# Moving work between three engines in the attention loops of a hybrid decoder trunk

## The reference, cut to what matters

```python
for layer in range(DEPTH):
    h = rms_norm(x, ln1_g[layer])
    (a_q, a_ckv, ..., b_u, c_q, c_kv, c_gate) = jnp.split(h @ w_in[layer], offsets, axis=-1)
    a_out = dsa_mixer(...)     # _, sel = lax.top_k(score, k_top), k_top = 64
    b_out = s5_mixer(...)      # y = gelu(Re(C h) + D u);  y * sigmoid(y @ glu_w + glu_b)
    c_out = nsa_mixer(...)
    x = x + mixed @ w_out[layer]
    z = rms_norm(x, ln2_g[layer]) @ w_up[layer]
    x = x + jnp.square(jax.nn.relu(z)) @ w_down[layer]
```

## Time and profile before

| | us |
|---|---|
| median of 3 runs | 635.5 (634.96 to 637.03) |
| profiled execution | 635.55 |
| its span, first to last instruction | 633.8 |
| PE busy | 611.7 (97%) |
| DVE busy | 437.0 (69%) |
| ACT busy | 360.5 (57%) |
| POOL busy | 237.8 (38%) |

### The profile page before, as it was taken

The page is one execution under the profiler, slowest core; times in us unless marked ns, Lnnn a source line. Parts: engine busy times, 40 slices in busy tenths (PEclk is TensorE's granted clock), DMA queues, the critical chain, the costliest instruction groups (busy, mean ns, idle before and its releaser), DMA issues.

```text
span 633.8 us, 10302 instructions
## 1 busy us (share of the span) xinstructions
PE 611.7 (97%) x3798; PEld 505.8 (80%) x3798; DVE 437.0 (69%) x785; ACT 360.5 (57%) x639; POOL 237.8 (38%) x418
## 2 busy tenths in 40 slices
PE   7989989999999999999999999999999999999996
PEld 6867866688888888888888787668888888888885
DVE  7699887396756767895676877637776654665664
ACT  5855689736546444444375658984654553554452
POOL 5899678504031999960005206871000000000001
PEclk9999999999999999999999999999999999999999
DMA  9674804165965655466638640414576656656631
GB/s 255 206 205 134 162 8 113 42 184 156 293 209 190 198 171 195 148 197 227 195 94 280 118 123 3 118 35 132 140 261 199 189 176 199 199 172 194 197 102 66
DMA packets 55436, 102.73 MB, mean 162 GB/s; under 512 B 12713, under 2 KB 18906, under 8 KB 55354
## 3 DMA queue, kind: packets, MB, share of 16 engines
q1 hardware_dynamic: 49130, 96.30, 50.3%
q0 software_dynamic: 1792, 4.07, 2.8%
q10 hardware_dynamic: 4464, 1.70, 1.1%
HBM read 99.69 MB, written 1.31 MB: 159 GB/s over the span
## 4 chain that ended last, share of the span: by engine, by line
PE 80%; POOL 6%; ACT 5%; DVE 5%; issue 2%; DMA 1%; SPq 0%; POOLq 0%; DVEq 0%; ACTq 0%
PE pb L1799 77%; ACT tab_zone L1172 2%; POOL dtmp L840 1%; DVE sc_zone L1687 1%; DMA raw<-in_w_in 1%; ACT w_hi L926 1%; POOL yz L621 1%; PE pb L1953 1%; PE pb L1825 1%; POOL sp L621 1%; DVE w_lo L1371 1%; ACT ptmp L1186 1%; PE pb L2219 1%; POOL w_lo L801 1%; DVE tab_zone L1292 1%
## 5 line engine op out<-in xcount | busy, mean ns | idle before, releaser
L1371 DVE TENSOR_TENSOR w_lo<-raw,w_hi 128x1024 fp32r<-128x1024 f32 (+2 forms) x176 | 221.6, 1268 | 124.3 <-ACT w_hi L926 123.5
L926 ACT ACTIVATE w_hi<-raw 128x1024 fp32r<-128x1024 f32 (+2 forms) x184 | 188.0, 1027 | 188.3 <-PE pb L1799 174.4
L1799 PE MATMUL pb<-h_both,w_hi 128*128 128x512 f32 x512 | 181.7, 399 | 0.0
L1799 PE MATMUL pb<-h_both,w_lo 128*128 128x256 f32 x512 | 143.7, 281 | 0.0
L1799 PE MATMUL pb<-w_hi,h_both 128*128 128x512 f32 (+2 forms) x448 | 128.0, 370 | 5.3 <-DVE w_lo L1371 5.2
L1799 PEld LDWEIGHTS pb<-h_both,w_hi 128*128 128x128 f32 x512 | 96.2, 188 | 24.2 <-issue 0.6
L1799 PE MATMUL pb<-w_hi,z_hi 128*128 128x512 f32 (+1 forms) x260 | 101.0, 388 | 0.4 <-DVE w_lo L1371 0.4
L1799 PE MATMUL pb<-w_lo,z_hi 128*128 128x512 f32 (+1 forms) x260 | 100.5, 387 | 0.0
L1799 PE MATMUL pb<-w_hi,z_lo 128*128 128x512 f32 (+1 forms) x260 | 100.5, 386 | 0.0
L1799 PEld LDWEIGHTS pb<-h_both,w_lo 128*128 128x128 f32 x512 | 96.7, 189 | 0.5
L1799 PEld LDWEIGHTS pb<-w_hi,h_both 128*128 128x128 f32 x448 | 78.9, 188 | 20.1 <-DVE w_lo L1371 6.9
(11 more groups left out here) (315 smaller groups left out, 801.5 us busy)
## 6 DMA issues: line engine op xcount, KB each, us to landing
raw<-in_w_up SPq DMA_DIRECT2D x64, 512.0 KB, 4.1
raw<-in_w_down SPq DMA_DIRECT2D x64, 512.0 KB, 3.4
raw<-in_w_in SPq DMA_DIRECT2D x24, 512.0 KB, 4.3
raw<-in_w_out SPq DMA_DIRECT2D x8, 512.0 KB, 3.6
raw<-in_w_out SPq DMA_DIRECT2D x16, 256.0 KB, 4.9
raw<-in_w_in SPq DMA_DIRECT2D x8, 308.0 KB, 4.0
raw<-in_w_in SPq DMA_DIRECT2D x8, 280.0 KB, 2.9
x<-in_x ACTq DMA_DIRECT2D x4, 256.0 KB, 4.7
```

What stands on the lines that cost most here:

```text
L926: hi_made.by(act.activation(w_hi[:, n % RING, 0:width(n)], raw[:, n % RING, 0:width(n)], ACT.Copy))
L1371: lo_made.by(dve.tensor_tensor(w_lo[:, n % RING, 0:width(n)], raw[:, n % RING, 0:width(n)], w_hi[:, n % RING, 0:width(n)].bitcast(F32), AL ...
L1799: return pe.matmul(o, l, r, start=start, stop=stop, skip_group_check=True)
```

## The change

Four edits:
1. In layer 0, `s5_states_back` leaves DVE and is run by POOL, between `keys_w` and `gates`, with a new signal `scanned` for the two scans. Layer 1 keeps it on DVE.
2. In layer 0, one of the two rounds of maxima of slot 2 goes to slot 0, which then has two.
3. In both layers, turned y is read from PSUM by DVE, in slot 7 (`y_read`), and not by ACT. In layer 0 it stands ahead of `c_probs`, in layer 1 `c_probs` is a slot earlier.
4. In layer 1, POOL makes the low part of piece 22 behind slot 6, not slot 3.

```diff
-        LO_OUT = (None, 1, 3, 7)
+        LO_OUT = ((None, 1, 3, 7), (None, 1, 6, 7))
...
+                def s5_states_back():
+
+                    P0, P1, P3 = (t.rearrange("p (i n) -> p i n", i=2)
+                                  for t in (dtmp[:, 4], dtmp[:, 5], proj[:, 1, O_U - 256:O_U + 256]))
+                    c2, s2 = (rot[:, i].rearrange("p j c -> p (j c)").unsqueeze(1).to_broadcast([PART, 2, SEQ])
+                              for i in range(2))
+                    pool.wait_ge(scanned.sem, 2)
+                    tt(P0, P3, c2, ALU.mult, False)
+                    tt(P1, P3, s2, ALU.mult)
+                    Q = [P.rearrange("p i (j c) -> p i j c", j=PAIRS)[:, :, :, 0:NC - 1] for P in (P0, P1)]
+                    tt(ez[:, 0, :, 1:NC], Q[0][:, 0], Q[1][:, 1], ALU.subtract, False)
+                    ez_made.by(pool.tensor_tensor(ez[:, 1, :, 1:NC], Q[1][:, 0], Q[0][:, 1], ALU.add))
+                    pool.wait_ge(ez_made.sem, ez_made.at(L, 1))
+
                 keys_w()
+                if L == 0:
+                    s5_states_back()
                 gates()
...
-                    if p in LO_OUT:
-                        lo_out(20 + LO_OUT.index(p))
+                    if p in LO_OUT[L]:
+                        lo_out(20 + LO_OUT[L].index(p))
...
-                    if p == 6:
-                        act.wait_ge(yk_ps.sem, yk_ps.at(L, 1))
-                        yk_sb.by(act.activation(yg, pb[7][:], ACT.Copy))
-                        yk_half.by(act.activation(yt, pb[7][:], ACT.Copy, scale=0.25))
...
-                        step(dve.tensor_tensor_scan(P[3][:, i], d, P[2][:, i], 0.0, ALU.mult, ALU.add), i == 1)
+                        m = dve.tensor_tensor_scan(P[3][:, i], d, P[2][:, i], 0.0, ALU.mult, ALU.add)
+                        if L == 0:
+                            scanned.by(m)
+                        else:
+                            step(m, i == 1)
...
+                def y_read():
+
+                    dve.wait_ge(yk_ps.sem, yk_ps.at(L, 1))
+                    yk_sb.by(dve.tensor_copy(yg, pb[7][:]))
+                    yk_half.by(dve.tensor_scalar(yt, pb[7][:], 0.25, None, ALU.mult))
+
...
-                              19: (s5_lags, s5_sums_read, s5_states, index_sum, s5_states_back)}
+                              19: (s5_lags, s5_sums_read, s5_states, index_sum)}
...
-                for p, work in ((3, y_cube), (4, y_gelu), (5, c_max), (6 + D, c_probs), (9, y_glu)):
+                for p, work in ((3, y_cube), (4, y_gelu), (5, c_max), (7, y_read), (6 + D, c_probs), (9, y_glu)):
                     between[p].append(work)
-                for p in ((0, 1, 2, 2, 3, 4, 5, 6) if L == 0 else (0, 0, 2)):
+                for p in ((0, 0, 1, 2, 3, 4, 5, 6) if L == 0 else (0, 0, 2)):
                     between[p].append(top)
```

More of the change, by code:

```diff
@@ L339, in trunk @@
         xs_read = sig("xs_read", 1)
-        ez_made = sig("ez_made", 1)
+        scanned, ez_made = sig("scanned", 0), sig("ez_made", 1)
         rk_ps = sig("rk_ps", 1)
```

## The result

| | before | after |
|---|---|---|
| median, first comparison | 635.71 (634.96 to 637.42, 7 runs) | 633.20 (632.82 to 634.20, 7 runs) |
| second comparison | 635.90 (25 runs) | 634.43 (632.77 to 636.49, 10 runs) |
| third | 635.94 (23 runs) | 633.89 (632.39 to 639.94, 11 runs) |
| profiled execution / span | 635.55 / 633.8 | 633.19 / 631.5 |

What follows compares the result with a forecast made beforehand. PE, busy for 97% of the span, was taken to bound the kernel. Gains of 0.4 us in layer 0 and 0.8 in layer 1, 1.2 off 635.5, gave 634.3; own range 634.1 to 635.1, 8-in-10 range 632.9 to 636.0.

Steps and rivals of the forecast that it cites:

- part 2: Layer 0, a maximum from slot 2 to slot 0: sc of slot 4 stays, sc of slot 5 gains 0.5 us.
- part 3: DVE reads turned y, 1.3 us: layer 0 keeps 0.4 of a 0.5 us gain; in layer 1 the reads cost nothing.
- the 0.4 of the sum: Layer 0's gain in us as taken for the forecast, with bounds 0 and 0.5.
- three signs of failure: Four S5 operations over 6.6 us; PE waiting for c_probs in layer 0's slot 8; layer 1's last transposes waiting for non-POOL.
- Part 1: Layer 0's S5 states on POOL: four operations take 4.0 us there, cost nothing, and alone gain nothing.
- the forecast 0.5 of waiting: Layer 0, sc of slot 5 loses its 0.51 us wait and goes to where DVE is free, 94.57.
- a cover of 0.1 us: Layer 0: c_probs ends at 104.95, PE turns its result at 105.08 when 0.5 early.
- Part 4: Layer 1, piece 22's low part from slot 3 to 6: last transposes go as POOL ends; 0.8 us taken.
- The bound of 0.9: Layer 1's upper gain in us, last transposes at 420.2 to 420.3; 0.4 if pn of slot 6 doesn't start earlier.
- all counts: Rival: all time taken away in both layers, 3.7 us, is gained, giving 631.8; chance 0.12.
- the waits move elsewhere: Rival: layer 0 gains 0 as c_probs is late for PE, layer 1 gains 0.4, giving 635.1; chance 0.20.
- POOL is held up: Rival: layer 0's four S5 operations take 11.6 us on POOL; 5.0 lost, 0.8 gained, giving 639.7; chance 0.08.

Runs made afterwards that it cites:

- e7: Kernel before with only layer 0's S5 states moved to POOL: 635.79 us, ratio 0.9979.
- e12: Kernel before with only the low part of layer 1's piece 22 moved to behind slot 6: 634.72 us (1 run).
- e13: Kernel before with one maximum of layer 0 moved from slot 2 to slot 0 and the table's loads issued ahead of the weights: 634.51 us (1 run).
- e2: Kernel before with turned y read by DVE in both layers and layer 1's piece 22 behind slot 6: 635.59 us, ratio 0.9990.
- e8: Changed kernel with two more 512-column products on DVE in slot 0 of layer 0: 634.65 us (1 run).
- e5: Kernel before, unchanged, profiled and timed again: 635.67 us.
- e9: Kernel before with the loads of layer 0's table of lags issued ahead of the weights on SP's queue: 636.94 us, ratio 0.9992.
- e14: Changed kernel with the table's loads first and two more products on DVE behind slot 2's scores in layer 0: 635.63 us.
- e10: Changed kernel with the loads of layer 0's table of lags issued ahead of the weights on SP's queue: 633.64 us, ratio 0.9938.
- e11: Changed kernel with the table's loads first and one more product on DVE behind slot 2's scores in layer 0: 634.63 us (1 run).
- e15: Changed kernel, unchanged, a third time: 633.89 us over eleven runs.
- e4: Changed kernel with the low part of layer 1's piece 22 behind slot 5 instead of 6: 633.70 us, ratio 0.9950.
- e16: Changed kernel with the table's loads first and layer 1's piece 22 in slot 5: 632.91 us, ratio 0.9940.

## Why the prediction was wrong in layer 0, and what in it was right

The step that failed is part 2's path through slots 3 and 4 of layer 0: sc of slot 4 "at 91.3, as before", and from there a gain of 0.5 us, less 0.1 for part 3. The measured loop gained 0.95 us for the 0.4 of the sum, 0.80 of it at the same lateness. Layer 1 gained 1.11 for 0.8, with the mechanism right and the size too small.

**What bounds the kernel, and the mechanisms.** These held. PE's wait before the scores of slot 4 went from 1.44 to 0.24; the last transposes of layer 1 are released by POOL; POOL has no gap from piece 22 on. None of the three signs of failure that it named came; they looked at POOL's price, c_probs and the end of layer 1, and none at the step that failed.

**Part 1** by itself gave nothing where it was tried, with a late table (e7, against e12), at 3.98 us for the 4.0. That it is only room for part 2 was right too; it is worth 0.44 where the table is early (e13).

**Part 2** is the step that failed. It had DVE's cube wait for ACT's square of y, which doesn't move, and so sc of slot 4 where it was. ACT hardly moved, but the square, which ended at 89.13, had not been what the cube waited for. Timeline of DVE in the kernel before, the cube in slot 3 and sc of slot 4:

```profile
89.36 0.68 DVE L1299 SCALAR_TENSOR_TENSOR yz<-yz,pb 128x512 f32<-128x512 f32 x1
...
91.34 0.28 DVE L1687 CUSTOM_DVE_ANT_0 sc_zone<-pb,cmask 128x128 f32<-128x128 f32 x1
```

The cube starts at 89.36 with no bracket: it stood in DVE's own queue, behind slot 3's sc, and that queue is what the change shortens. In after it has a bracket, 0.91 for ACT, and starts at 89.02, 0.34 earlier: 0.20 of the 0.23 us that lay between the square's end and the cube's start, and 0.14 because the square itself was that much earlier, as PE was (its product with the table at 80.81 and not 80.94). The same 0.33 stands at sc of slot 4 (91.01 for 91.34). The sum hid it: cube and top are 1.98 us in this timeline, from 89.36 to 91.34, where 0.65 and 1.45, 2.10, had been added to 89.13 and came out near the old time. DVE then took 3.15 us to sc of slot 5, where 3.23 had passed before, and the forecast 0.5 of waiting went as well: 94.16, 0.92 before the 95.08 of the earlier trace rows, and 0.93 of it reached the last transposes. The loop, by the table above, takes 37.43 us in the kernel before with a lateness of 0 or 0.33, and 36.75 and the lateness with 1.26 or 1.47 (e7, e12); the two meet at about 0.7, an estimate, as no profile lies between. In the changed kernel it is 36.30 and the lateness. At before's own 0.33 that is a gain of 0.80, twice the 0.4 of the sum, of which 0.1 had been taken off for part 3. With a late table it is 0.45, near the size forecast, but by luck: in e12 DVE stood 0.73 us for PE ahead of sc of slot 2, so the late table had already given DVE time.

**Part 3** was right in its price (0.66 and 0.68, for 1.3) and wrong in what it uses up: 0.1 was taken off for a cover of 0.1 us ahead of PE's turning of c_probs. c_probs ended at 104.50, 0.45 us earlier than forecast, after sc of slot 5 that was 0.41 earlier than forecast; PE, at 104.64, didn't wait for it, and e2 shows 21.96 against 21.97. In layer 1, too, it is nothing (e12).

**Part 4** went as told to a tenth: in before's time pn of slot 6 is at 407.74 (407.75 forecast), piece 22 at 409.68 (409.7), pn of slot 7 at 412.02 (412.05). The last transposes are at 420.06, where 420.2 was worked out and 0.8 taken of the 0.97 that it meant. It measured 1.11; the difference is 0.14 of overlap between POOL's operations, and the rounding down. The bound of 0.9 was too tight for a sum over six operations. The later load of piece 26 cost nothing that shows: from the last transposes to the end of the span it is 212.68 us for 212.63.

**The rivals.** That all counts (631.8) didn't come, nor that the waits move elsewhere (635.1). That POOL is held up (639.7) didn't come either, and e8 gives the price beside two wide products on DVE: 4.73 us for the four operations, below its point of 6.6.

**What the prediction did not weigh** is that executions of the kernel before differ by what happens in this very stretch. With an early table its layer 0 has a wait of 1.67 to 1.77 us before the scores of slot 4, and the clock over 90 to 95 us was then 0.66 in two of three profiles (e5, e2; not in e9), which cost 1.56 us (38.99 against 37.43). It was 1.00 in e14 with 1.83, and in all 14 with 1.44 or less. So the wait alone doesn't decide it. Something sets e2 and e5 apart from e9 and e14 that the experiments left untried: an earlier fall of the clock. (e9's expectation named a late start of the layer as a rival; e2 and e5 came to slot 1 at 79.25 and 79.32 us, e9 and e14 at 78.44 and 78.72.) The window from 10 us on, in e5 and then in e9:

```profile
core 0: us, PE busy (x) PEld busy (x) DVE busy (x) ACT busy (x) POOL busy (x), PEclk, DMA share, GB/s
10.00:15.00 5.00, 3.34 (x11) 2.57 (x10) 4.37 (x8) 5.00 (x11) 3.96 (x10) 0.68 1.22 306
```

```profile
core 0: us, PE busy (x) PEld busy (x) DVE busy (x) ACT busy (x) POOL busy (x), PEclk, DMA share, GB/s
10.00:15.00 5.00, 3.07 (x13) 2.55 (x14) 4.60 (x8) 5.00 (x11) 3.88 (x10) 1.00 1.22 299
```

Six of the 18 profiles have a clock below 1.00 somewhere in 10 to 20 us: after, e2, e5, e10, e11 and e15. Both falls at 90 us are among these, with the long wait. The other four of them waited 0.24 to 1.10 us, and e9 and e14 had the long wait without the earlier fall; in none of these six did the clock fall over 90 to 95 us. That would fit a cause that needs both, but two profiles of each kind don't show it, and no run tried it. The timed runs don't settle it either. e9 against e10, on one chip, looks like a fall in half of the executions that have the wait. But on e14's chip four of e14's ten runs had a granted clock of 0.995 or less, and so did five of e15's eleven, which don't have the wait. A run's clock doesn't tell where it fell; in after, e4 and e16 it was 0.94, 0.85 and 0.73 over 625 to 630 us.

What the profiles do show is 0.45 to 1.13 us in layer 0, by the lateness of the table, and 1.0 to 1.1 in layer 1, 1.5 to 2.3 together. The medians give 2.5, 1.5 and 2.0 us; the first is above this, and the three intervals (1.7 to 4.7, 0.8 to 3.9 and 0.4 to 3.6 us) reach into it. How much of the rest is the clock stays open.

## What to carry to other kernels

When work leaves an engine, ask of each later operation whether it waited for another engine or for its own queue; the bracket in the trace tells only the last to come, and an operation without a bracket stood in its own queue and moves. Take a second profile of the kernel before, before costing an edit at half a microsecond: here the lateness of a table and the clock were worth as much as the edit. A chain over many small operations deserves a bound wider than its rounding.

## What the hardware showed that I had not expected

- What was issued ahead of the table's loads on SP's queue set when they landed: the slowest took 6.4 to 8.4 us behind three loads of weights (12 profiles), 4.2 to 4.7 without them (6 profiles), first issued at 70.0 to 71.1 us in both.
- The kernel before had TensorE at a mean of 0.66 of full clock over 90 to 95 us in one profile (e5, after a wait of 1.67 us) and, with one line moved on SP's queue, at 1.00 in another (e9, after 1.77).
- Two wide SBUF products on DVE beside two on POOL cost DVE 3.21 us for 1.35, POOL 2.97 for 2.53.
